# Attention stages: a third score buffer, the maxima reordered on VectorE and the exponentials reordered on ScalarE

## The chip, the cores and the metric

The kernel runs on one core of a Trainium2 chip. The metric is device time in microseconds of one execution. TensorE, VectorE (DVE), ScalarE (ACT), GpSimd (POOL) and SyncE (SP) each run their own instruction queue in order and meet at semaphores.

## The reference, cut to what matters

Two transformer blocks are applied to 512 latent tokens of width 1024, the first with 256 context tokens beside them. All is float32. Four attentions are computed: a neighbourhood attention in each layer of the first block (with an attention among the context tokens in the first layer only), then a differential attention and a forgetting attention in the second block.

```python
# neighbourhood: local keys with a bias table, and all 256 context keys
s_loc = einsum('bjqhd,bjkhd->bhjqk', q_r, k_loc) * scale + bias
p = softmax(concatenate([s_loc, s_ctx], -1), -1)
out = p[..., :n_loc] @ v_loc + p[..., n_loc:] @ v_ctx
# differential: 8 heads, two softmaxes each, causal
logits = einsum('bqhmd,bkhmd->bhmqk', qb, k) * scale + bias
p = softmax(where(rel >= 0, logits, -inf)); w = p[:, :, 0] - lam * p[:, :, 1]
o = rms_norm(w @ v, subln_g) * (1 - lambda_init)
# forgetting: 16 heads, causal, with a decay that is added to the scores
logits = einsum('bqhd,bkhd->bhqk', qb, k) * scale + decay
out = softmax(where(causal, logits, -inf)) @ v
```

Around them stand projections, a gated recurrence, expert layers and dense layers with matrices of 1024 by up to 5632.

## The kernel before, in words

All four attentions are built by one function, `attention` (line 1260). Its work is cut into units. A unit is 128 queries of two heads (or of the two halves of one differential head), against nk keys. In the neighbourhood stages nk is 512 in 12 units per layer, and the first layer has six more units, for the context tokens, with nk of 256. The differential and the forgetting stages have 32 units each; nk goes 128, 256, 384, 512, 512, 384, 256, 128 and again, so that 8 units are one cycle.

One unit goes through these steps:

1. scores (TensorE, L1295), into one of two pairs of PSUM banks. Unit u+2 waits until VectorE has taken the scores of unit u.
2. maxima (VectorE): the `pre` of the stage (L1453 and L1454; L2692 and L2694; L2875 and L2878) moves the scores with their bias into the score buffer S, then L1384 reduces them to a negated maximum.
3. exponentials (ScalarE, L1345), in place in S, with their sum.
4. transposes (TensorE, L1306), in one or two rounds of up to four tiles of 128x128. Round 0 goes into one PSUM bank, round 1 into another. Each round waits until the copies of the preceding unit have emptied its bank.
5. copies (ScalarE, L1362), one per round, from PSUM to the buffer ET.
6. product with the values (TensorE, L1323 with L1326, or L1330 in the differential stage). L1326 also spreads the reciprocals of the sums (VectorE, L1390).
7. output: ScalarE copies the spread reciprocals (L1354) and VectorE multiplies (L1408). In the differential stage VectorE does both steps itself (L2698, L2699).

The order of each queue is written out by hand. TensorE does, for each u: transposes of u, scores of u+2, product of u-1. ScalarE does: copies of u, exponentials of u+1, reciprocal copy of u-1, then the extra work of the stage. VectorE does: reciprocals of u-1, maxima of u+1, output of u-2, then the extra work.

Only the differential stage has extra work, for the norm over each head. After the fourth unit of a head VectorE clamps that head's outputs (`on_dve`, L2749) for unit u-4; ScalarE squares them (`on_act`, `squares`, L2724) for unit u-3, and waits for the clamp. ScalarE then takes roots (L2729 to L2731) every second head and scales the finished outputs (`scaled`, L2737, four instructions per head) in two later places.

Of the kernel before, what the change touches and what calls it, by code (L numbers as in the profile page):

```python
# [22 lines left out]
P = 128  # L23
D = 1024
KT = D // P
NLAT, NCTX = 512, 256
NTOK = NLAT + NCTX
# [7 lines left out]
LOCAL = 2 * NA_ROWS * BLOCK  # L35
BIAS_KINDS = 3
BIAS_PAIR = HEADS_PER_TILE * BIAS_KINDS * LOCAL
# [170 lines left out]
def build(nc, wtile, wahead, wmod, wshift, conds, params, consts, rope, onehot, biases, x_in, out, dbg=None, dbg_name="X", upto=99, limit=10 ** 9):  # L208
    with ExitStack() as ctx:
# [8 lines left out]
        X = sb_split("X", KT * NTOK)  # L218
        H = sb_split("H", 8192)
        ring = sb_split("ring", SLOTS * TILE)  # L220
        PB = sb_split("PB", 23552)
# [15 lines left out]
        bank = [psum[:, 512 * i:512 * i + 512] for i in range(8)]  # L237
# [81 lines left out]
        ident = cn("ident", 0, P)  # L319
# [940 lines left out]
        def attention(units, S, ET, stats, sc_sets, turn_banks, odd_on_act=False, outputs=None):  # L1260
# [4 lines left out]


            n = len(units)
            NS = len(sc_sets)
            B = lambda s, k=n: s.reserve(k)
            b_sr, b_tk = B(scores_ready), B(scores_taken)  # L1270
            b_mx, b_ex, b_or, b_oc = B(max_ready), B(exp_ready), B(out_ready), B(out_copied)
# [11 lines left out]
            scale = lambda u: small[:, u % 2 * P:(u % 2 + 1) * P]  # L1283
            mx = lambda u: stats[:, 2 * u:2 * u + 2]
            sm = lambda u: stats[:, 2 * (n + u):2 * (n + u) + 2]
            Sv = lambda u: S[u % 2][:, 0:2 * units[u]["nk"]].rearrange("p (m k) -> p m k", m=2)
            copied = lambda r, u: (probsT_copied.sem, b_ca + n_a[u] + r // 2 + 1) if r % 2 == 0 else (hidT_copied.sem, b_cd + n_d[u] + r // 2 + 1)

            def scores(eng, u):
# [8 lines left out]
            def ten(eng, ready, values):  # L1298
                def turn(u):
                    eng.wait_ge(exp_ready.sem, b_ex + u + 1)  # L1300
                    for r, tiles in enumerate(rounds(u)):
                        ready, before = ((probsT_ready, n_a[u]), (hidT_ready, n_d[u]))[r % 2]
                        if before + r // 2:
                            eng.wait_ge((probsT_copied, hidT_copied)[r % 2].sem, (b_ca, b_cd)[r % 2] + before + r // 2)
                        for t in tiles:
                            mm = nc.tensor.transpose(bank[tb[r % 2]][:, (t % 4) * P:(t % 4) * P + P], S[u % 2][:, t * P:(t + 1) * P], ident)  # L1306
                        mm.then_inc(ready.sem, 1)

                def product(u):
                    if u < 0:  # L1310
                        return
                    for r in range(len(rounds(u))):
                        eng.wait_ge(*copied(r, u))
                    if u >= 2:
                        eng.wait_ge(out_copied.sem, b_oc + u - 1)
                    if u == 0:
                        values(eng)
                    nt, w = units[u]["nk"] // P, units[u]["width"]
                    probs = lambda m, t: ET[u % 2][:, (m * nt + t) * P:(m * nt + t + 1) * P]
                    if turned[u]:  # L1320
                        for t in range(nt):
                            for m in range(2):
                                nc.tensor.matmul(ob(u)[64 * m:64 * m + 64, 0:P], units[u]["pv"](m, t), probs(m, t), start=(t == 0), stop=(t == nt - 1))  # L1323
                        eng.wait_ge(recip_ready.sem, b_rc + u + 1)
                        for m in range(2):
                            mm = nc.tensor.matmul(ob(u)[64 * m:64 * m + 64, P:2 * P], sm(u)[:, m:m + 1].broadcast_to([P, DH]), ident, start=True, stop=True)  # L1326
                    else:
                        for m in range(2):
                            for t in range(nt):
                                mm = nc.tensor.matmul(ob(u)[:, m * w:(m + 1) * w], probs(m, t), units[u]["pv"](m, t), start=(t == 0), stop=(t == nt - 1))  # L1330
                    mm.then_inc(out_ready.sem, 1)
                ready(eng)
                scores(eng, 1)
                for u in range(n):
                    turn(u)
                    scores(eng, u + 2)
                    product(u - 1)
                product(n - 1)
# [9 lines left out]
            def sca(eng):  # L1348
                def copy_scale(u):
                    if u >= 0 and turned[u]:  # L1350
                        if u >= 2:
                            eng.wait_ge(out_copied.sem, b_oc + u - 1)
                        eng.wait_ge(out_ready.sem, b_or + u + 1)
                        nc.scalar.copy(scale(u), ob(u)[:, P:2 * P]).then_inc(scale_copied.sem, 1)  # L1354
                for u in range(n):
                    for r, tiles in enumerate(rounds(u)):
                        if r % 2 == 0 or odd_on_act:
                            ready, copied_, first = ((probsT_ready, probsT_copied, b_ta + n_a[u]), (hidT_ready, hidT_copied, b_td + n_d[u]))[r % 2]
                            eng.wait_ge(ready.sem, first + r // 2 + 1)
                            if u >= 2:  # L1360
                                eng.wait_ge(out_ready.sem, b_or + u - 1)
                            nc.scalar.copy(ET[u % 2][:, tiles[0] * P:(tiles[-1] + 1) * P], bank[tb[r % 2]][:, 0:len(tiles) * P]).then_inc(copied_.sem, 1)  # L1362
                    exponentials(eng, u + 1)
                    copy_scale(u - 1)
                    if outputs is not None and u >= 3:
                        outputs[0](eng, u - 3)
                copy_scale(n - 1)
                if outputs is not None:
                    for u in range(n - 3, n):
                        outputs[0](eng, u)  # L1370
                    outputs[2](eng)

            def maxima(eng, u):
                if u >= n:
                    return
                if u >= 2:
                    if n_a[u - 1]:
                        eng.wait_ge(probsT_ready.sem, b_ta + n_a[u - 1])
                    if n_d[u - 1]:
                        eng.wait_ge(hidT_ready.sem, b_td + n_d[u - 1])  # L1380
                eng.wait_ge(scores_ready.sem, b_sr + u + 1)
                units[u]["pre"](eng, Sv(u), sets(u)).then_inc(scores_taken.sem, 1)
                eng.wait_ge(scores_taken.sem, b_tk + u + 1)
                nc.vector.tensor_reduce(mx(u), Sv(u), AX, ALU.max, negate=True).then_inc(max_ready.sem, 1)  # L1384

            def vec(eng):
                for u in range(n + 2):
                    if 1 <= u <= n:
                        eng.wait_ge(exp_ready.sem, b_ex + u)
                        nc.vector.reciprocal(sm(u - 1), sm(u - 1)).then_inc(recip_ready.sem, 1)  # L1390
                    if u < n:
                        maxima(eng, u + 1)
                    if u < n:
                        for r, tiles in enumerate(rounds(u)):
                            if r % 2 and not odd_on_act:
# [4 lines left out]
                    if u >= 2:  # L1400
                        x = u - 2
                        w = units[x]["width"]
                        eng.wait_ge(out_ready.sem, b_or + x + 1)
                        if turned[x]:
                            eng.wait_ge(scale_copied.sem, b_sc + n_t[x] + 1)
                            dst = units[x]["dst"]
                            flat = (lambda ap: ap) if len(dst.shape) == 2 else (lambda ap: ap.rearrange("p (r c) -> p r c", c=BLOCK))
                            ins = nc.vector.tensor_tensor(dst, flat(ob(x)[:, 0:P]), flat(scale(x)), ALU.mult)  # L1408
                        else:
                            eng.wait_ge(recip_ready.sem, b_rc + x + 1)  # L1410
                            ins = units[x]["out"](eng, ob(x)[:, 0:2 * w].rearrange("p (m e) -> p m e", m=2), sm(x))
                        ins.then_inc(out_copied.sem, 1)
                    if outputs is not None and u >= 4:
                        outputs[1](eng, u - 4, b_oc + u - 3)
                if outputs is not None:
# [5 lines left out]
            return (lambda eng: scores(eng, 0)), (lambda eng: exponentials(eng, 0)), (lambda eng: maxima(eng, 0)), run  # L1421


        SN = [PB[:, 2 * NTOK:2 * NTOK + 4 * LOCAL], X[:, 2 * BIAS_PAIR:2 * BIAS_PAIR + 4 * LOCAL]]
        EN = [PB[:, 4 * NTOK:4 * NTOK + 4 * LOCAL], H[:, KT * NTOK:KT * NTOK + 4 * LOCAL]]
        far_banks = lambda bs: psum[:, 512 * bs[0]:512 * bs[0] + 1024].rearrange("p (m k) -> p m k", m=2)[:, :, LOCAL:LOCAL + NCTX]
        two_banks = lambda bs, nk: psum[:, 512 * bs[0]:512 * bs[0] + 1024].rearrange("p (m k) -> p m k", m=2)[:, :, 0:nk]
# [1235 lines left out]

        QK2 = lambda i: PB[:, i * NLAT:(i + 1) * NLAT]
        V2 = PB[:, 8192:8192 + 4096].rearrange("p (t n) -> p t n", t=4)
        S3 = [PB[:, 16384 + b * 2 * NLAT:16384 + (b + 1) * 2 * NLAT] for b in range(2)]
        ET3 = [PB[:, 18432 + b * 2 * NLAT:18432 + (b + 1) * 2 * NLAT] for b in range(2)]
        BT2 = PB[:, 20480:20480 + 2048].rearrange("p (h n) -> p h n", h=A_HEADS)
        OTOK = H[:, 0:4096].rearrange("p (j n) -> p j n", j=4)
        SQ = H[:, 4096:4608].rearrange("p (j n) -> p j n", j=4)  # L2670
        KV = PB[:, 11776:11776 + 8192]
        O4 = PB[:, 4096:8192].rearrange("p (k t) -> p k t", k=KT)
        S4 = [PB[:, 8192 + b * 2 * NLAT:8192 + (b + 1) * 2 * NLAT] for b in range(2)]
        ET4 = [PB[:, 20480 + b * 2 * NLAT:20480 + (b + 1) * 2 * NLAT] for b in range(2)]
        FK = [PB[:, 22528:23552].rearrange("p (h k) -> p h k", h=2), H[:, 0:(B_HEADS - 2) * NLAT].rearrange("p (h k) -> p h k", h=B_HEADS - 2)]
        FQ = X[:, NLAT:NLAT + 4 * B_HEADS].rearrange("p (j h) -> p j h", j=4)
# [442 lines left out]
```

## Time and profile before

| | us |
|---|---|
| median of 3 runs | 3840.16 (3836.74 to 3841.09) |
| profiled execution, its own time | 3846.45 |
| its span, first to last instruction | 3844.7 |
| TensorE busy | 3605.9 (94%) |
| VectorE busy | 2157.3 (56%) |
| ScalarE busy | 1569.2 (41%) |
| chain that ended last | TensorE 83%, DVE 6%, ACT 4%, DMA 3%, issue 2% |

The four attention stages take some 287 us of the span together. In the views, a row of instructions has its busy time and the idle time of its engine just before it, with what released it. PE is TensorE's matmul queue.

### The profile page before, as it was taken

How to read it: one execution, taken by the hardware profiler on the slowest of the kernel's cores; microseconds unless marked ns; L12 is line 12 of the kernel's file. 1: busy time of each engine (PE TensorE's matmuls, PEld its weight loads, DVE VectorE, ACT ScalarE, POOL GpSimd, SP SyncE). 2: the span in 40 equal slices, each digit the busy share in tenths (PEclk: the TensorE clock that was granted, in tenths of full speed). 3: DMA queues.
4: the chain of work that ended last, by engine and by line, in shares of the span. 5: the costliest groups of instructions: out<-in, count | busy, mean ns of one | idle time of the engine just before them, and what ended most of it. 6: DMA issues, size and time to landing. Idle time of an engine off the chain costs nothing.

```text
span 3844.7 us, 51787 instructions
## 1 busy us (share of the span) xinstructions
PE 3605.9 (94%) x19796; PEld 2766.0 (72%) x19796; DVE 2157.3 (56%) x3269; ACT 1569.2 (41%) x2667; POOL 307.0 (8%) x410
## 2 busy tenths in 40 slices
PE   8998897999999687999999998999999999889998
PEld 7886574666788454556888776788878887667887
DVE  7867845987785773337763346666234333664332
ACT  3336634988423762113222346322233222553222
POOL 0110001100111002001210000111000001000001
PEclk9999578999999668999999999999999999999999
DMA  7552013998456017996773210576323223312222
GB/s 276 175 172 97 2 61 128 373 349 315 164 203 189 1 45 273 406 405 240 271 245 107 99 61 17 191 235 204 103 88 137 93 99 104 132 39 88 98 97 74
DMA packets 166268, 620.69 MB, mean 161 GB/s; under 512 B 19116, under 2 KB 20741, under 8 KB 164893
## 3 DMA queue, kind: packets, MB, share of 16 engines
q1 hardware_dynamic: 114928, 420.58, 30.3%
q0 software_dynamic: 46880, 169.11, 13.3%
q10 hardware_dynamic: 4238, 27.90, 1.9%
q8 instruction: 157, 2.57, 0.3%
q14 instruction: 65, 0.53, 0.0%
HBM read 596.74 MB, written 17.88 MB: 160 GB/s over the span
## 4 chain that ended last, share of the span: by engine, by line
PE 83%; DVE 6%; ACT 4%; DMA 3%; issue 2%; SPq 0%; POOL 0%; DVEq 0%; ACTq 0%; POOLq 0%
PE psum L2594 24%; PE psum L886 13%; PE psum L2608 13%; PE psum L983 5%; PE psum L2200 4%; PE psum L1059 4%; PE psum L813 3%; DMA ring<-wtile 2%; PE psum L2431 2%; PE psum L2219 2%; PE psum L2450 1%; PE psum L1306 1%; PE psum L1295 1%; PE psum L821 1%; PE psum L1585 1%
## 5 line engine op out<-in xcount | busy, mean ns | idle before, releaser
L837 ACT CAST small_r<-ring 128x1024 fp32r<-128x1024 f32 x263 | 275.0, 1048 | 1034.8 <-PE psum L886 336.4
L841 DVE TENSOR_TENSOR ring_r<-ring,small_r 128x1024 fp32r<-128x1024 f32 x264 | 322.7, 1224 | 645.6 <-ACT small_r L837 645.3
L837 ACT CAST PB_r<-ring 128x1024 fp32r<-128x1024 f32 x247 | 256.4, 1049 | 544.1 <-PE psum L2594 325.2
L841 DVE TENSOR_TENSOR ring_r<-ring,PB_r 128x1024 fp32r<-128x1024 f32 x248 | 299.5, 1222 | 246.8 <-ACT PB_r L837 246.3
L2594 PE MATMUL psum<-H_r,ring_r 128*128 128x512 f32 x1344 | 336.2, 392 | 0.0
L2594 PE MATMUL psum<-H_r,small_r 128*128 128x512 f32 x1344 | 326.9, 395 | 0.0
L2594 PE MATMUL psum<-H_r,PB_r 128*128 128x512 f32 x1344 | 318.6, 389 | 0.0
L2594 PEld LDWEIGHTS psum<-H_r,small_r 128*128 128x128 f32 x1344 | 252.3, 188 | 61.2
L2594 PEld LDWEIGHTS psum<-H_r,ring_r 128*128 128x128 f32 x1344 | 252.2, 188 | 56.0
L2594 PEld LDWEIGHTS psum<-H_r,PB_r 128*128 128x128 f32 x1344 | 252.3, 188 | 53.4
L886 PE MATMUL psum<-H_r,small_r 128*128 128x512 f32 (+1 forms) x944 | 251.8, 365 | 0.0
L886 PEld LDWEIGHTS psum<-H_r,small_r 128*128 128x128 f32 x944 | 159.0, 188 | 32.5 <-issue 1.8
L2608 PE MATMUL psum<-PB_r,ring_r 128*128 128x512 f32 x704 | 177.3, 392 | 0.0
L2608 PE MATMUL psum<-PB_r,small_r 128*128 128x512 f32 x704 | 171.9, 395 | 0.0
L886 PE MATMUL psum<-X_r,small_r 128*128 128x512 f32 x624 | 170.8, 344 | 0.0
L2608 PE MATMUL psum<-PB_r 128*128 128x512 f32 x704 | 167.7, 389 | 0.0
L886 PE MATMUL psum<-H_r,ring_r 128*128 128x512 f32 (+1 forms) x784 | 160.3, 353 | 0.0
L2634 DVE TENSOR_TENSOR small<-small,psum 128x512 f32<-128x512 f32 x88 | 60.5, 688 | 172.8 <-PE psum L2594 171.3
L2608 PEld LDWEIGHTS psum<-PB_r,small_r 128*128 128x128 f32 x704 | 132.1, 188 | 32.0
L2608 PEld LDWEIGHTS psum<-PB_r,ring_r 128*128 128x128 f32 x704 | 132.1, 188 | 29.3
L2608 PEld LDWEIGHTS psum<-PB_r 128*128 128x128 f32 x704 | 132.1, 188 | 28.2
L886 PEld LDWEIGHTS psum<-H_r,ring_r 128*128 128x128 f32 x784 | 128.2, 188 | 21.8
(472 smaller groups left out, 6561.5 us busy)
## 6 DMA issues: line engine op xcount, KB each, us to landing
ring<-wtile SPq DMA_DIRECT2D x776, 512.0 KB, 5.4
spare<-wmod POOLq DMA_DIRECT2D x97, 512.0 KB, 4.7
H<-wmod POOLq DMA_DIRECT2D x48, 512.0 KB, 4.5
PB<-wmod POOLq DMA_DIRECT2D x48, 512.0 KB, 4.4
X<-wmod POOLq DMA_DIRECT2D x47, 512.0 KB, 5.1
PB<-wahead POOLq DMA_DIRECT2D x16, 512.0 KB, 7.9
h_rows<-PB POOLq DMA_DIRECT2D x10, 512.0 KB, 4.4
PB<-wmod SPq DMA_DIRECT2D x4, 1024.0 KB, 15.2
```

The source lines that it names most:

```text
L813: nc.tensor.matmul(out(j, w)[:, 0:e - a], halves[j][z][:, k * P:(k + 1) * P], src[1][0](k, a, e), start=(x == 0 and z == 0), stop=False)
L837: copy(high(j), slot(g0 + j)).then_inc(high_ready.sem, 1)
L841: nc.vector.tensor_tensor(low(g0 + j), slot(g0 + j), high(j).bitcast(F32), ALU.subtract).then_inc(low_ready.sem, 1)
L886: mm = nc.tensor.matmul(bank[b + w][:, 0:e - a], w_part[:, k * P:(k + 1) * P], src[1][x](k, a, e), start=(not last and k == 0 and x == 0), ...
L983: mm = nc.tensor.matmul(bank[ob(c, t)][:, 0:width], src[1][x](2 * q + k, t * P, (t + 1) * P), w_part[:, 512 * k:512 * k + width], start=(j ...
L1059: mm = nc.tensor.matmul(bank[2 * (j % 2) + w][:, 0:e - a], w_part[:, k * P:(k + 1) * P], parts_at[1][x](k, a, e), start=(not last and k == ...
L2200: mm = nc.tensor.matmul(bank[2 + s][0:M, :], XG[x][:, 2 * q + k, 0:M], w_part[:, 512 * k:512 * k + 512], start=(not low and q == 0 and k = ...
L2219: mm = nc.tensor.matmul(bank[6 + s][0:M, :], HIDT[x][:, f, 0:M], w_part[:, 512 * s:512 * s + 512], start=(not low and f == 0 and x == 0), ...
L2431: mm = nc.tensor.matmul(bank[2 + s][M * o:M * o + M, 0:HALF], XG[e % 2][:, 2 * q + k, :], w[:, EXP_DIM * k + HALF * o:EXP_DIM * k + HALF * ...
L2594: mm = nc.tensor.matmul(bank[2 * (p % 2) + z][:, :], w_part[:, k * P:(k + 1) * P], SLIM[1][x](k, 0, NLAT), start=(not last and k == 0 and ...
L2608: mm = nc.tensor.matmul(bank[4 + j % 2][:, :], w_part[:, k * P:(k + 1) * P], HID2[x][:, kk * NLAT:(kk + 1) * NLAT], start=(not last and kk ...
L2634: nc.vector.tensor_tensor(SGF[p % 2], SGF[p % 2], bank[2 * (p % 2) + 1][:, :], ALU.mult).then_inc(prod_ready.sem, 1)
```

## The change

Four things are changed. Nothing else differs, and the count of compute instructions is the same.

- The score buffer S has three parts in place of two, in all four stages. The maxima of unit u then wait for the transposes of unit u-3, not u-2, before they write S.
- VectorE's maxima of unit 1 stand ahead of its loop. In the loop the maxima of u+1, which stood behind the reciprocals and ahead of the output of u-2, are replaced by those of u+2, behind that output and ahead of the stage's extra work.
- ScalarE's exponentials of u+1 stand ahead of its copies of u. They stood behind them.
- TensorE's order is the same: only the buffer that its transposes read is picked by `u % NB`.

```diff
-            NS = len(sc_sets)
+            NS, NB = len(sc_sets), len(S)
...
-            Sv = lambda u: S[u % 2][:, 0:2 * units[u]["nk"]].rearrange("p (m k) -> p m k", m=2)
+            Sv = lambda u: S[u % NB][:, 0:2 * units[u]["nk"]].rearrange("p (m k) -> p m k", m=2)
...
                 for u in range(n):
+                    exponentials(eng, u + 1)
                     for r, tiles in enumerate(rounds(u)):
...
-                    exponentials(eng, u + 1)
                     copy_scale(u - 1)
...
-                if u >= 2:
-                    if n_a[u - 1]:
-                        eng.wait_ge(probsT_ready.sem, b_ta + n_a[u - 1])
-                    if n_d[u - 1]:
-                        eng.wait_ge(hidT_ready.sem, b_td + n_d[u - 1])
+                if u >= NB:
+                    if n_a[u - NB + 1]:
+                        eng.wait_ge(probsT_ready.sem, b_ta + n_a[u - NB + 1])
+                    if n_d[u - NB + 1]:
+                        eng.wait_ge(hidT_ready.sem, b_td + n_d[u - NB + 1])
...
             def vec(eng):
+                maxima(eng, 1)
                 for u in range(n + 2):
                     if 1 <= u <= n:
                         eng.wait_ge(exp_ready.sem, b_ex + u)
                         nc.vector.reciprocal(sm(u - 1), sm(u - 1)).then_inc(recip_ready.sem, 1)
-                    if u < n:
-                        maxima(eng, u + 1)
...
                         ins.then_inc(out_copied.sem, 1)
+                    maxima(eng, u + 2)
                     if outputs is not None and u >= 4:
                         outputs[1](eng, u - 4, b_oc + u - 3)
...
-        SN = [PB[:, 2 * NTOK:2 * NTOK + 4 * LOCAL], X[:, 2 * BIAS_PAIR:2 * BIAS_PAIR + 4 * LOCAL]]
+        SN = [PB[:, 2 * NTOK:2 * NTOK + 4 * LOCAL], X[:, 2 * BIAS_PAIR:2 * BIAS_PAIR + 4 * LOCAL], X[:, 2 * BIAS_PAIR + 4 * LOCAL:2 * BIAS_PAIR + 8 * LOCAL]]
...
-        S3 = [PB[:, 16384 + b * 2 * NLAT:16384 + (b + 1) * 2 * NLAT] for b in range(2)]
+        S3 = [PB[:, a:a + 2 * NLAT] for a in (16384, 16384 + 2 * NLAT, 12288)]
...
-        S4 = [PB[:, 8192 + b * 2 * NLAT:8192 + (b + 1) * 2 * NLAT] for b in range(2)]
+        S4 = [PB[:, 8192 + b * 2 * NLAT:8192 + (b + 1) * 2 * NLAT] for b in range(3)]
```

## Rows read from the trace of the kernel before

**Rows 1.** Windows of the four attention stages: length, busy time of each engine, clock.
```profile
316.28:372.30 56.02, 53.14 (x588) 40.42 (x588) 40.98 (x80) 42.95 (x118) 1.34 (x2) 0.97 0.23 79
1242.60:1284.30 41.70, 39.75 (x458) 31.79 (x456) 30.82 (x56) 31.48 (x80) 0.00 (x0) 0.96 0.15 50
2268.00:2364.00 96.00, 87.91 (x604) 64.90 (x604) 80.28 (x197) 73.95 (x259) 0.00 (x0) 0.96 0.02 7
3315.50:3409.00 93.50, 77.55 (x730) 50.86 (x728) 78.42 (x186) 65.51 (x204) 0.00 (x0) 0.98 0.11 44
```

**Rows 2.** Timeline, neighbourhood stage, first layer: start, duration, engine, line, idle before.
```profile
326.90 0.73 ACT L1345 ACTIVATE X<-X,spare 128x512 f32<-128x512 f32 x1
...
328.23 0.20 ACT L1345 ACTIVATION_READ_ACCUMULATOR X<-X,spare 128x1 f32 x1
...
328.59 1.09 PE L1306 MATMUL psum<-con,X 128*128 128x128 f32 x8
...
329.29 1.07 ACT L1362 COPY H<-psum 128x512 f32<-128x512 f32 x2 [0.31 <-PE psum L1306]
...
329.62 1.15 PE L1295 MATMUL psum<-PB,H 64*128 64x128 f32 x12
...
330.24 0.73 ACT L1345 ACTIVATE PB<-PB,spare 128x512 f32<-128x512 f32 x1
...
330.91 0.69 DVE L1453 TENSOR_SCALAR X<-psum 128x512 f32<-128x512 f32 x1 [0.46 <-PE psum L1295]
...
332.24 1.22 DVE L1384 TENSOR_REDUCE spare<-X 128x2 f32<-128x1024 f32 x1
...
333.59 0.73 ACT L1345 ACTIVATE X<-X,spare 128x512 f32<-128x512 f32 x1
```

**Rows 3.** Windows: four context units, one differential cycle, one forgetting cycle.
```profile
360.61:369.89 9.28, 7.75 (x79) 5.12 (x77) 5.70 (x15) 7.20 (x25) 0.00 (x0) 1.00 0.01 3
2317.55:2340.45 22.90, 21.46 (x155) 16.04 (x153) 20.38 (x52) 19.57 (x73) 0.00 (x0) 1.00 0.00 1
3340.91:3362.95 22.04, 19.29 (x185) 12.59 (x185) 20.05 (x49) 16.55 (x52) 0.00 (x0) 1.00 0.01 1
```

**Rows 4.** Groups by line in the forgetting cycle: count, busy, mean ns, idle before.
```profile
L1345 ACT ACTIVATE PB<-PB,spare 128x128 f32<-128x128 f32 (+3 forms) x16 | 8.9, 557 | 1.5 <-DVE spare L1384 1.5
L2875 DVE SCALAR_TENSOR_TENSOR PB<-H,X,psum 128x256 f32<-128x256 f32 (+3 forms) x16 | 8.0, 541 | 1.4 <-PE psum L1295 1.2
L1384 DVE TENSOR_REDUCE spare<-PB 128x2 f32<-128x256 f32 (+3 forms) x8 | 6.6, 820 | 0.3
...
L1306 PE MATMUL psum<-con,PB 128*128 128x128 f32 x41 | 6.4, 285 | 2.8 <-ACT PB L1345 2.6
...
L1362 ACT COPY PB<-psum 128x512 f32<-128x512 f32 (+1 forms) x12 | 5.8, 516 | 3.3 <-PE psum L1306 3.1
L2878 DVE TENSOR_TENSOR PB<-PB,con 128x256 f32<-128x256 f32 x9 | 3.8, 425 | 0.3
```

**Rows 5.** Timeline of the forgetting stage: a late load, and a unit with nk of 128.
```profile
3327.01 1.41 DVE L2875 SCALAR_TENSOR_TENSOR PB<-H,X,psum 128x512 f32<-128x512 f32 x2 [2.92 <-DMA H<-frow_save]
...
3342.72 0.44 PE L1306 MATMUL psum<-con,PB 128*128 128x128 f32 x2
...
3343.09 0.92 PE L1295 MATMUL psum<-PB 64*128 64x384 f32 x4
...
3359.05 0.49 PE L1295 MATMUL psum<-PB 64*128 64x128 f32 x4
```

**Rows 6.** Groups by line in the differential cycle (columns as in the forgetting cycle).
```profile
L2694 DVE SCALAR_TENSOR_TENSOR PB<-psum,PB 128x512 f32<-128x512 f32 (+1 forms) x9 | 5.6, 621 | 0.2
...
L2724 ACT ACTIVATE H<-H 128x128 f32<-128x128 f32 x9 | 2.7, 296 | 0.2
...
L2692 DVE TENSOR_SCALAR PB<-psum,PB 128x256 f32<-128x256 f32 (+1 forms) x4 | 2.4, 598 | 0.0
...
L2749 DVE TENSOR_SCALAR H<-H 128x512 f32<-128x512 f32 x2 | 0.8, 422 | 0.0
```

More of the change, by code:

```diff
@@ L1305, in turn @@
                         for t in tiles:
-                            mm = nc.tensor.transpose(bank[tb[r % 2]][:, (t % 4) * P:(t % 4) * P + P], S[u % 2][:, t * P:(t + 1) * P], ident)
+                            mm = nc.tensor.transpose(bank[tb[r % 2]][:, (t % 4) * P:(t % 4) * P + P], S[u % NB][:, t * P:(t + 1) * P], ident)
                         mm.then_inc(ready.sem, 1)
```

## The prediction

> **What bounds the kernel now.** I read the windows of the four attention stages first. They last 56.0, 41.7, 96.0 and 93.5 us [rows 1]; the change touches nothing else, so 287 of 3844.7 us are at stake. TensorE is busy for 95%, 95%, 92% and 83% of them, VectorE for 73% to 84%, ScalarE for 70% to 77%. No engine is full, so the period of a unit is set by loops of waits through several engines, and the sum has to be made over these loops.
>
> The timeline of the neighbourhood stage shows them [rows 2]. The reader is to see three things in it.
>
> First, the period: exponentials start at 326.90, 330.24 and 333.59, one unit every 3.34 us.
>
> Second, a loop over one unit. The exponentials start at 326.90 and end at 328.43 (1.53). The transposes start 0.16 later, at 328.59. The copies start 0.70 behind them, at 329.29. The next exponentials start 0.95 behind the start of the copies, at 330.24. The sum is 3.34, the period itself. The copies stand in this loop because the exponentials are queued behind them. Call it loop A.
>
> Third, a loop over two units, B: scores, maxima, exponentials, transposes, scores. Maxima from 330.91 to 332.24+1.22=333.46 take 2.55; 0.13 later the exponentials start, at 333.59, though 0.04 would do as I read it from the shortest gaps. Exponentials take 1.53, then 0.16 to the transposes; from there 1.03 to the scores (328.59 to 329.62); scores take 1.15 and 0.14 pass to the maxima (329.62+1.15=330.77 to 330.91). That is 2.55+0.04+1.53+0.16+1.03+1.15+0.14=6.60 for two units, 3.30 per unit. Loop A is longer than B by only 0.04 per unit.
>
> **The change part by part.** *Third buffer and the maxima's wait.* The removed wait is for the transposes of u-2. But the scores of u are issued on TensorE behind the transposes of u-2, and the maxima need these scores anyway. The wait that ends last there is for the scores (0.46 us for L1295) [rows 2], so the buffer gives nothing: 0. It would give something only if TensorE's scores were issued earlier, and their order is unchanged. At the worst it costs nothing either, as it adds no instruction.
>
> *Maxima one place on.* Written as one sequence, VectorE did output u-2, reciprocals u, maxima u+2, output u-1. Now it does output u-2, maxima u+2, reciprocals u, output u-1. Only the reciprocals of u (0.15) and the extra work change sides. The maxima no longer wait for the exponentials of u, but they wait for the scores of u+2, which come behind the transposes of u, which wait for the same exponentials. So nothing is gained: 0. The reciprocals are late by one set of maxima; they are needed only at the end of the product of u, behind the transposes of u+1 and the scores of u+3, over 2 us later. Covered: 0. The extra work of the differential stage is priced below.
>
> *Exponentials ahead of the copies.* Loop A is cut: the exponentials no longer stand behind the copies. But now the copies of u-1 stand behind the exponentials of u. The transposes of u write the bank that these copies empty, so they wait for exponentials of u and then for the first copy of u-1. That lengthens loop B by a copy. This is the step that the prediction rests on.
>
> Neighbourhood stages: the copies' queue slot begins 1.42 to 1.43 behind the start of the exponentials (the read of the sum overlaps by 0.1), and two copies take 1.07 [rows 2], so one about 0.59, then 0.16 to TensorE as before: 2.17 in place of 1.53+0.16=1.69, +0.48. Loop B is 7.08, or 3.54 per unit against 3.34: +0.20. With 10 to 11 periods of full width per layer that is +2.1 per layer, +4.2 for both. Bounds: 0, if the copy starts before the exponentials do in some way that I don't see; +5.9 per layer if both copies (1.07) come into the loop. I take the first copy alone, because the second bank's transposes come half a microsecond later too. The six context units have a period of 9.28/4=2.32 [rows 3], and a chain with narrower terms; I take 0 for them, between -1 and +1.
>
> Forgetting stage, in cycles of 8 units, 22.04 us each [rows 3]. Loop B passes over every second unit, so over a cycle it holds half of each group. Exponentials 8.9/2=4.45; L2875 8.0/2=4.0; L2878 4x0.425=1.7, with 0.07 of gaps per unit 0.3; reduction 6.6/2=3.3; copies one per unit 4x0.516=2.1 [rows 4]. Transposes up to the scores 1.03 for 8 tiles [rows 2] and 0.37 for 2 (3342.72 to 3343.09) [rows 5], on average 0.70, x4=2.8. Scores 1.13 to 1.15 at the widest [rows 2] and 0.49 at the narrowest [rows 5], on average 0.81, x4=3.25. Handovers 0.15+0.04+0.10 per unit, x4=1.15. The sum is 23.05 against 22.04: +1.0 per cycle. Without the copy it would be about 21, below the present period, which shows that loop A bounds now. The stage has another brake: VectorE waits 2.92 us for a load at 3327 [rows 5], which comes at its own time and swallows what was lost before. That leaves 28 of 32 units, 3.5 cycles: +3.4. Bounds: 0; and +6.6 if the second copies count too (another 0.9 per cycle).
>
> Differential stage, 22.90 us per cycle [rows 3]. The same sum: exponentials 4.45, L2694 and L2692 together 4x0.92=3.7 (8 of the one, 4 of the other, 4.97+2.39=7.36, halved), reduction 3.3, copies 2.1, transposes 2.9, scores 3.25, handovers 1.15: 20.85. That alone would not bound. But here the extra work meets the new order. Squares of a finished head stand on ScalarE, in the iteration u=4h+3, and wait for the clamp on VectorE; the clamp now stands behind the maxima of u+2, and the exponentials of that same unit u+2=4h+5 stand behind the squares. So each head puts clamp and squares in series into loop B, always in the odd units: 0.42 less an overlap of 0.09, 0.04 of handover, and 4x0.296=1.18 [rows 6], together 1.55, twice per cycle: 3.1. One of the two sets of scalings per cycle (four instructions, taken at the length of the squares, 1.2) falls ahead of an odd unit's exponentials too. 20.85+3.1+1.2=25.15 against 22.90, and against 22.6 in a cycle without scalings: +2.4 per cycle, x3.5=+8.5. Bounds: +0, if squares find their operand in time; +12, if even units are held as well.
>
> *Sum:* 4.2+3.4+8.5=+16.1 us. The stages follow one another on TensorE and nothing runs beside them that could swallow it. Against the profiled execution that is 3846.45+16.1=3862.6. The median of the runs shown is 6.3 lower, so **3856.3**.
>
> **The rivals.** *Faster.* TensorE waits for the exponentials ahead of its transposes, 2.6 us per forgetting cycle [rows 4]. If the new order lets them start sooner and the bank is free in time, most of it goes: 2.6x3.5=9.1, and about as little again in the other stages, where TensorE is nearly full [rows 1]. With 10 us gained the time is 3830. It decides where the exponentials of u are done before the transposes of u-1 end, so that the copies of u-1 are never held. For it: VectorE and ScalarE have slack. Against: the maxima end only 0.13 us before the exponentials start now [rows 2], so they cannot start sooner. The Trainium skill, "Perfetto Trace Analysis", section Optimization Strategy, says that a gap that repeats on the engine that should be full can mean too few buffers for the next tile. By that rule the third buffer would bring this rival's 3830; what the trace shows before the gap is the exponentials, not a buffer.
>
> *Absorbed.* The copy's place matters less than the loop says, because waits overlap: within 4 us of before, 3842.
>
> *Bank only.* The copy costs what I say, the squares do not: +4.2+3.4 and up to 3 in the differential stage, 3849. It decides if the clamp is done by the time ScalarE's queue reaches the squares.
>
> *More.* The longer waits of TensorE lower its granted clock in parts of a stage. It is at 1.00 in three steady stretches in spite of waits [rows 3], and 0.96 to 0.98 over whole stages [rows 1], so against it. If half a cycle of each of the two long stages ran at 1.2 GHz, some 11 us would be added: 3867. The Trainium skill, "TensorE: Matmul & The Clock Gate", section "A second HAM failure mode: psum-queue depth-cycling", tells of such a fall between short bursts of matmuls.
>
> **How the numbers follow.** Forecast 0.56, bank only 0.19, more 0.08, absorbed 0.09, faster 0.08. The forecast's own range is 3850 to 3863. Below 3844 lie faster and most of absorbed, above 3867 half of the last: 3844 to 3867. About 0.2%, 7.7 us, is what a measurement can tell from no change: slower by more, 3847.9 and above, holds the forecast, more and most of bank only, 0.81; the same 0.11; faster 0.08.
>
> **What would show it.** In the neighbourhood stage the exponentials should start every 3.54 us on average over two units, and the transposes should follow the end of a copy, not of the exponentials. A forgetting cycle should last 23.0, a differential cycle 25.2. ScalarE should wait for L2749 ahead of L2724 twice per cycle. If TensorE's transposes start with no ScalarE wait, or the differential cycle stays below 23, the prediction is wrong. The rest of the kernel should keep its times.

## The result and the profile after

The changed kernel takes 3859.47 us (median of 5 runs, 3848.28 to 3864.54), the kernel before 3840.16 (5 runs, 3836.74 to 3844.6). The ratio is 1.0045, with a 95% interval of 1.0029 to 1.0061: slower by 11 to 23 us. The forecast was 3856.3. The profiled execution took 3863.77 us, with a span of 3862.0; forecast for it was 3862.6.

The windows of the four attention stages, now cut in the same way at rows of transposes (in the forgetting stage a little past the last), answer to [rows 1]; the columns are the same.

```profile
317.96:373.88 55.92, 50.13 (x551) 38.38 (x549) 40.13 (x77) 40.08 (x113) 0.27 (x1) 0.97 0.21 73
1244.01:1283.97 39.96, 36.35 (x411) 28.66 (x409) 30.08 (x53) 28.37 (x75) 0.00 (x0) 0.96 0.16 55
2276.61:2376.50 99.89, 85.57 (x589) 63.48 (x588) 78.34 (x186) 69.81 (x244) 0.00 (x0) 0.97 0.01 1
3330.05:3425.00 94.95, 77.96 (x730) 51.27 (x728) 78.55 (x187) 63.27 (x203) 0.00 (x0) 0.96 0.10 41
```

Measured in the same way in both traces, from the start of the first row of transposes to the start of the last, the stages took:

| us | neighbourhood 1 | neighbourhood 2 | differential | forgetting | sum |
|---|---|---|---|---|---|
| before | 52.5 | 38.1 | 90.5 | 91.5 | 272.6 |
| changed | 55.9 | 40.0 | 99.9 | 93.2 | 289.0 |
| difference | +3.4 | +1.9 | +9.4 | +1.7 | +16.4 |
| forecast | +2.1 | +2.1 | +8.5 | +3.4 | +16.1 |

The span grew by 17.3, so 0.9 lies elsewhere, and that is a small sum of larger things that have nothing to do with the change (see the last section). That the sums agree to 0.3 us is luck: the stages are off by +1.1, +0.9 and -1.7 (the two neighbourhood stages taken together).

The timeline of the neighbourhood stage in the changed kernel answers to [rows 2]. L1363 are the copies, L1362 before.

```profile
336.24 0.72 ACT L1345 ACTIVATE X<-X,spare 128x512 f32<-128x512 f32 x1 [0.95 <-DVE spare L1384]
...
337.67 1.04 ACT L1363 COPY PB<-psum 128x512 f32<-128x512 f32 x2
...
338.38 1.06 PE L1306 MATMUL psum<-con,X 128*128 128x128 f32 x8 [0.21 <-ACT PB L1363]
...
339.37 1.15 PE L1295 MATMUL psum<-PB,H 64*128 64x128 f32 x12
...
339.65 0.72 ACT L1345 ACTIVATE PB<-PB,spare 128x512 f32<-128x512 f32 x1 [0.77 <-DVE spare L1384]
...
340.67 0.69 DVE L1453 TENSOR_SCALAR X<-psum 128x512 f32<-128x512 f32 x1 [0.79 <-PE psum L1295]
```

The reader is to see the new loop B. Exponentials start at 336.24, the copies of the unit before them 1.43 later, and the transposes at 338.38, released by the copy and no longer by the exponentials: 2.14 behind the start of the exponentials, where it was 1.69 and the forecast 2.17. Scores follow 0.99 later, the maxima at 340.67. And ScalarE waits for the maxima, 0.95 and 0.77 us: it did not wait for them before, as its copies filled that time.

Three cycles as in [rows 3]: one of the forgetting stage, and the second and third of the differential stage.

```profile
3356.38:3379.36 22.98, 19.05 (x185) 12.58 (x185) 20.06 (x49) 16.06 (x53) 0.00 (x0) 1.00 0.01 1
2300.43:2325.70 25.27, 21.37 (x154) 16.04 (x153) 20.41 (x50) 17.30 (x63) 0.00 (x0) 1.00 0.01 1
2325.70:2352.55 26.85, 22.96 (x154) 16.71 (x153) 20.65 (x52) 19.54 (x71) 0.00 (x0) 0.94 0.00 1
```

Forecast were 23.0 and 25.2. The groups by line of the forgetting cycle answer to [rows 4].

```profile
L1345 ACT ACTIVATE PB<-PB,spare 128x256 f32<-128x256 f32 (+3 forms) x16 | 8.8, 554 | 6.4 <-DVE spare L1384 6.4
...
L1306 PE MATMUL psum<-con,PB 128*128 128x128 f32 x41 | 6.3, 280 | 4.1 <-ACT PB L1363 3.8
...
L1363 ACT COPY PB<-psum 128x512 f32<-128x512 f32 (+1 forms) x12 | 5.6, 498 | 0.0
```

TensorE waits 3.8 us per cycle for copies, where it waited 2.6 for exponentials. The copies wait for nothing, since they are queued behind exponentials that outlast the transposes. The exponentials wait 6.4 us for maxima in place of 1.5. In the second differential cycle, with the two lines in question:

```profile
L1306 PE MATMUL psum<-con,PB 128*128 128x128 f32 x40 | 5.8, 275 | 3.9 <-ACT PB L1363 3.9
...
L2724 ACT ACTIVATE H<-H 128x128 f32<-128x128 f32 x8 | 2.4, 297 | 3.0 <-DVE H L2749 3.0
```

ScalarE's squares wait 3.0 us per cycle for the clamp; before it was 0.2 [rows 6].

### The profile page after: what moved, and what is told of

It reads as the page before. It is cut to its first block, busy times and chain, and to the rows that moved or that the text cites. A ratio compares the mean times of both kernels' runs of the same rounds, so it can differ in the third digit from the quotient of the medians.

```text
span 3862.0 us, 51782 instructions
## 1 busy us (share of the span) xinstructions
PE 3600.8 (93%) x19796; PEld 2763.4 (72%) x19796; DVE 2158.9 (56%) x3269; ACT 1564.4 (41%) x2667; POOL 310.1 (8%) x410
## 4 chain that ended last, share of the span: by engine, by line
PE 81%; DVE 7%; ACT 5%; DMA 4%; issue 2%; SPq 0%; DVEq 0%; POOL 0%; ACTq 0%; POOLq 0%
PE psum L2594 24%; PE psum L886 13%; PE psum L2608 13%; PE psum L983 5%; PE psum L1059 4%; PE psum L2200 4%; DMA ring<-wtile 3%; PE psum L813 3%; PE psum L2431 2%; PE psum L2219 2%; PE psum L1295 1%; PE psum L2450 1%; PE psum L1306 1%; PE psum L821 1%; DVE spare L1384 1%
```

## The experiments

My theory has two parts. The first copy, put behind the exponentials, lengthens the loop over two units (loop B). The clamp, put behind the maxima, holds squares and with them exponentials in the differential stage. The rivals give it all to one of the two orders, to the buffer, or to ScalarE's load. Whole times of one kernel scatter by 10 us and more (before: 3833 to 3856 in 31 runs). From the second cycle on, a cycle repeats to 0.01 us between the two traces of the kernel before; in the changed kernel the third differential cycle, in which TensorE's clock fell, was 26.85 and 26.48. So the verdicts rest on cycles. In the fences below, the windows are six neighbourhood periods (five where the text says so), a differential cycle (the second, or the second and the third) and a forgetting cycle, as far as shown, with the columns of [rows 3]. The repeat of the kernel before is the yardstick; it comes first.

**The kernel before again.**

> The kernel before once more, for the scatter of its parts between executions: cycles 3.35, 22.9 and 22.04 us again to 0.1 us; if TensorE's clock rises at another time in the first recurrence, that part differs by several us with nothing changed.

```profile
333.77:353.85 20.08, 20.08 (x243) 16.06 (x241) 16.67 (x31) 16.50 (x42) 0.00 (x0) 1.00 0.01 2
2302.05:2324.66 22.61, 21.45 (x154) 16.04 (x153) 20.09 (x52) 17.31 (x63) 0.00 (x0) 1.00 0.01 2
2324.66:2347.56 22.90, 21.46 (x154) 16.04 (x153) 20.38 (x52) 19.56 (x73) 0.00 (x0) 1.00 0.00 1
3350.17:3372.20 22.03, 19.29 (x186) 12.59 (x185) 20.05 (x49) 16.55 (x52) 0.00 (x0) 1.00 0.01 1
```

Periods of 20.08/6=3.35, cycles of 22.61, 22.90 and 22.03: the same to 0.01, in an execution that was 8 us longer as a whole (3854.13).

**VectorE's part alone.** The diff is against the changed kernel, as in all that follow but where said.

```diff
                 for u in range(n):
-                    exponentials(eng, u + 1)
                     for r, tiles in enumerate(rounds(u)):
...
+                    exponentials(eng, u + 1)
                     copy_scale(u - 1)
```

> The change without its ScalarE part: exponentials of u+1 behind the copies of u again; third buffer and VectorE's new order kept. Theory of the two loops: loop A is back and bounds the neighbourhood and forgetting stages as before, 3.34 us per unit of full width and 22.0 per forgetting cycle. In the differential stage the clamp still stands behind the maxima of u+2, so squares wait: the cycle between 24 and 26 us, total 6 to 9 us above before. Rival 'ScalarE's order is all of it': differential cycle 22.6 to 22.9, total as before within 2 us.

```profile
2283.16:2308.53 25.37, 21.68 (x155) 16.08 (x154) 20.33 (x50) 17.51 (x63) 0.00 (x0) 1.00 0.01 1
```

Six neighbourhood periods take 20.08 us and the forgetting cycle 22.04, as before. The second differential cycle is 25.37, the third 26.31 (25.27 and 26.85 in the changed kernel): nearly all of its differential loss, with ScalarE's order as before. The ratio of the whole is 1.0017 (1.0003 to 1.0030), 1 to 12 us, with 6 to 9 expected. The rival that ScalarE's order is all of it is out.

**ScalarE's part alone.**

```diff
             def vec(eng):
-                maxima(eng, 1)
...
+                    if u < n:
+                        maxima(eng, u + 1)
...
                         ins.then_inc(out_copied.sem, 1)
-                    maxima(eng, u + 2)
```

> The change without its VectorE part: maxima of u+1 in their old place; third buffer and the exponentials ahead of the copies kept. Theory of the two loops: neighbourhood 3.5 per unit and forgetting 23.0 per cycle as in the changed kernel; differential 23.3 to 24.2 per cycle, as the clamp stands in its old place; total about 11 above before. Rival 'the maxima's order is all of it': 3.34, 22.9 and 22.0, total as before within 2 us. Rival 'the ScalarE order alone costs as much as the whole change': differential cycle 25 or more, total 16 above.

```profile
331.97:353.05 21.08, 20.32 (x240) 16.04 (x241) 16.75 (x31) 15.83 (x43) 0.00 (x0) 1.00 0.01 4
2293.82:2317.02 23.20, 21.42 (x154) 16.04 (x153) 20.25 (x52) 17.02 (x63) 0.00 (x0) 1.00 0.01 1
...
3341.37:3364.35 22.98, 19.05 (x184) 12.58 (x185) 19.80 (x49) 16.04 (x53) 0.00 (x0) 1.00 0.00 1
```

21.08/6=3.51 and 22.98: the whole loss of the neighbourhood and forgetting stages comes from ScalarE's order. The second differential cycle is 0.6 above before, a bit below the 23.3 that I gave as the low end; the third is 23.60. The whole time is a miss: ratio 0.9997 (0.9982 to 1.0013), at most 5 us slower, where I expected 11. The stages of its trace add up to 9.4 us more than before (54.3, 42.5, 91.6 and 93.6), of which some 3 are in the start of the second stage. Where the rest of the whole time gives that back was not found; the scatter of its other parts is as large.

**The third buffer alone.** Both orders put back as in the two runs above.

> The third score buffer alone, both orders as before. Theory: nothing, since the scores come behind the same transposes that free the buffer: 3.34, 22.9 and 22.0 us, total as before but for the scatter of the clock in the recurrence. Rival 'the buffer's place in memory costs': single instructions of L1384, L1345 or L1306 longer than 1220, 714 and 273 ns in their widest forms and the cycles longer by that. Rival 'buffer helps': cycles shorter by 0.2 us or more.

```profile
331.50:351.58 20.08, 20.08 (x243) 16.06 (x241) 16.67 (x31) 16.52 (x42) 0.00 (x0) 1.00 0.02 7
2283.87:2306.48 22.61, 21.45 (x154) 16.04 (x153) 20.09 (x52) 17.32 (x63) 0.00 (x0) 1.00 0.01 1
...
3331.45:3353.48 22.03, 19.29 (x186) 12.59 (x184) 19.69 (x48) 16.56 (x52) 0.00 (x0) 1.00 0.01 1
```

Nothing, to 0.01 us, in these windows; the ratio is 0.9995 (0.9982 to 1.0007). The next cycle of either stage is a little longer than before, 23.02 against 22.90 and 22.39 against 22.04; why was not looked into. None is shorter.

**The changed kernel with the clamp ahead of the maxima.**

```diff
-                    maxima(eng, u + 2)
                     if outputs is not None and u >= 4:
                         outputs[1](eng, u - 4, b_oc + u - 3)
+                    maxima(eng, u + 2)
```

> The changed kernel with VectorE's extra work of the differential stage (the clamp, L2749) ahead of the maxima of u+2 in place of behind. Theory: the squares no longer wait for a whole set of maxima, the differential cycle falls from 26.8 to 23.3 to 24.2; neighbourhood and forgetting stages as in the changed kernel, 3.5 and 23.0; total about 11 above before, 6 below the changed kernel. Rival 'the squares do not matter, only the copy behind the exponentials': the differential cycle stays at 25 to 27 and the total at that of the changed kernel.

The second and third differential cycle (the forgetting cycle is 22.99, as in the changed kernel):

```profile
2292.84:2315.99 23.15, 21.44 (x155) 16.05 (x154) 20.21 (x51) 17.03 (x63) 0.00 (x0) 1.00 0.01 1
2315.99:2339.56 23.57, 21.42 (x154) 16.04 (x153) 20.68 (x52) 19.66 (x73) 0.00 (x0) 1.00 0.00 1
```

One moved line takes the stage from 99.9 to 91.6 us; the squares' wait for the clamp falls from 3.0 us in the second cycle to 0.8. So the clamp's place costs 8.3 us. Against the given trace of the kernel before, 1.1 would be left for the copy behind the exponentials, but that trace ran at half clock at the start of this stage, and its repeat did not:

```profile
2270.57:2277.30 6.73, 6.30 (x21) 3.00 (x20) 4.34 (x9) 3.35 (x10) 0.00 (x0) 0.52 0.00 0
2279.10:2285.80 6.70, 5.10 (x30) 2.67 (x28) 5.59 (x10) 4.03 (x12) 0.00 (x0) 1.00 0.01 4
```

The first differential cycle took 24.36 us in the one and 22.97 in the other. By the cycles the copy costs 0.5 to 0.7 (23.15 against 22.61, 23.57 against 22.90), an estimate of some 2 us for 3.5 cycles. The ratio to before is 1.0005 (0.9990 to 1.0020), -4 to +8 us, where I expected 11: a miss, as with ScalarE's part alone.

**The first copy ahead of the exponentials.** This tells the first copy from ScalarE's load.

```diff
                 for u in range(n):
-                    exponentials(eng, u + 1)
...
                             nc.scalar.copy(ET[u % 2][...], bank[tb[r % 2]][...]).then_inc(copied_.sem, 1)
+                            if r == 0:
+                                exponentials(eng, u + 1)
```

> The changed kernel with one thing moved: ScalarE's exponentials of u+1 stand between the first and the second copy of u, in place of ahead of both. VectorE's order, the clamp behind the maxima, TensorE's order and the third buffer are as in the changed kernel. Theory that the first copy behind the exponentials is what lengthens loop B: neighbourhood back to 3.34 us per unit, forgetting cycle to 22.0 or a little less; the differential cycle keeps the cost of the clamp and stays at 24.5 to 26. Rival 'it is ScalarE's load or any copy behind the exponentials': 3.5 and 23.0 stay.

```profile
333.94:354.02 20.08, 20.08 (x243) 16.06 (x241) 16.59 (x31) 16.85 (x43) 0.00 (x0) 1.00 0.01 2
2296.33:2321.25 24.92, 21.74 (x154) 16.03 (x153) 20.32 (x50) 17.52 (x63) 0.00 (x0) 1.00 0.00 1
...
3350.39:3372.22 21.83, 19.34 (x186) 12.55 (x184) 19.96 (x49) 16.60 (x52) 0.00 (x0) 1.00 0.01 2
```

3.35, and 21.83, 0.2 below before: with one copy moved past the exponentials the loss is gone, and the differential stage keeps the clamp's (24.92, then 25.89). Both parts of the theory stand. This kernel was executed once (3854.16 us), so its whole time says nothing.

**Scores ahead of the transposes.** The theory says what the third buffer could be good for: loop B runs through the scores only because TensorE issues them behind the transposes. The clamp stands ahead of the maxima here.

```diff
                 for u in range(n):
-                    turn(u)
                     scores(eng, u + 2)
+                    turn(u)
                     product(u - 1)
```

> The changed kernel with the clamp ahead of the maxima, and on TensorE the scores of u+2 issued ahead of the transposes of u in place of behind them. Theory: this is what the third buffer and the early maxima lacked. Loop B (scores, maxima, exponentials, copy, transposes, scores) is cut, as the scores wait only until VectorE has taken those of u. Neighbourhood 3.1 to 3.25 us per unit in place of 3.51, forgetting cycle 21.0 to 21.5 in place of 22.98, differential 22.2 to 22.8 in place of 23.6; in all about 9 us below the kernel before. Rival 'the copies behind the exponentials bound by themselves, whatever TensorE does': cycles stay at 3.5, 23.0 and 23.6.

```profile
332.59:349.32 16.73, 16.73 (x202) 13.38 (x200) 14.15 (x25) 13.68 (x36) 0.00 (x0) 1.00 0.02 6
2291.73:2313.99 22.26, 20.58 (x154) 15.94 (x153) 19.75 (x50) 16.96 (x63) 0.00 (x0) 1.00 0.01 2
...
3337.15:3358.28 21.13, 19.37 (x187) 12.54 (x185) 19.81 (x49) 15.77 (x52) 0.00 (x0) 1.00 0.01 2
```

The differential and the forgetting cycle fall below the kernel before: 22.26 and 21.13. The neighbourhood period does not. The first window holds five periods, 16.73/5=3.35, where I expected 3.1 to 3.25. TensorE is busy for all of it, as it is for all of the 20.08 us of the kernel before, so it is the bound in both. The exponentials are now far ahead of it:

```profile
333.37 0.19 ACT L1345 ACTIVATION_READ_ACCUMULATOR X<-X,spare 128x1 f32 x1
...
335.94 1.09 PE L1306 MATMUL psum<-con,X 128*128 128x128 f32 x8
```

They end at 333.56, 2.38 us before the transposes that read them (0.16 in [rows 2]), and the period is the same. What the neighbourhood stages gain (49.3 against 52.5 us for the first) lies in the first units and in the last two of full width, which take 2.90 us each there. The ratio is 0.9981 (0.9967 to 0.9995).

**The same with the exponentials between the copies.** The diff is against the run just told of.

```diff
                 for u in range(n):
-                    exponentials(eng, u + 1)
...
                             nc.scalar.copy(ET[u % 2][...], bank[tb[r % 2]][...]).then_inc(copied_.sem, 1)
+                            if r == 0:
+                                exponentials(eng, u + 1)
```

> As the run with the scores first, but ScalarE's exponentials of u+1 stand between the first and the second copy of u. Theory: the first copy is never held by exponentials, and in the differential and forgetting stages that gains: cycles 21.8 to 22.3 and 20.8 to 21.3; in the neighbourhood stage the copy comes back into the path, 3.2 to 3.3 us per unit; in all about 10 us below the kernel before. Rival: the two places are alike, as every wait is covered once the scores come first; all cycles within 0.1 of those of the run with the scores first.

```profile
2286.81:2308.57 21.76, 20.82 (x154) 15.90 (x152) 19.75 (x50) 17.32 (x65) 0.00 (x0) 1.00 0.01 2
...
3329.70:3350.38 20.68, 19.54 (x186) 12.50 (x184) 19.55 (x49) 15.96 (x52) 0.00 (x0) 1.00 0.01 2
```

0.5 less per cycle in both causal stages. The neighbourhood period is again 3.35, with TensorE busy throughout (3.2 to 3.3 expected). Median 3829.79, ratio 0.9970 (0.9954 to 0.9985): 6 to 18 us below before.

**Scores first in the kernel before.** The diff is against the kernel before; the third buffer is added as in the change.

```diff
-            NS = len(sc_sets)
+            NS, NB = len(sc_sets), len(S)
...
                 for u in range(n):
-                    turn(u)
                     scores(eng, u + 2)
+                    turn(u)
```

> The kernel before with three buffers and TensorE's scores of u+2 ahead of the transposes of u; ScalarE and VectorE in their old orders. Theory: loop A (exponentials behind the copies, copies behind the transposes) is not cut: the neighbourhood stage stays at 3.33 to 3.35 us per unit; the forgetting cycle falls to 21.3 to 21.7, as VectorE no longer waits for scores; total 3 to 5 us below before. Rival 'loop B bounded alone, so that scores first is enough': neighbourhood 3.1 to 3.25.

```profile
332.18:348.92 16.74, 16.74 (x203) 13.39 (x201) 13.84 (x25) 13.21 (x35) 0.00 (x0) 1.00 0.03 12
```

Five neighbourhood periods of 3.35, as expected, but this does not show loop A: TensorE is busy for all of the 16.74 us, so its own work sets the period here too. The forgetting cycle is 21.16, the second differential cycle 21.79. The ratio is 0.9973 (0.9958 to 0.9988); 3 to 5 us were expected and 5 to 16 were measured. So most of the gain comes with TensorE's order, without the changed orders of the other two.

**The better place in each stage.** Exponentials ahead of both copies in the neighbourhood stages, between them elsewhere. The diff is against the run with the exponentials between.

```diff
                 for u in range(n):
+                    if not between:
+                        exponentials(eng, u + 1)
...
-                            if r == 0:
+                            if r == 0 and between:
                                 exponentials(eng, u + 1)
```

> Scores first and the clamp first in all stages; exponentials ahead of both copies in the neighbourhood stages, between the copies in the differential and forgetting stages. Theory: each stage as in the better of the two runs before: first transposes to last 49.3, 35.6, 84.2 and 85.8 us; that is 1.4 us below the run with the exponentials between everywhere, about 14 below the kernel before in the stages, of which the whole time shows 9 to 15. Rival: stages lean on one another, the first one's gain is taken back in the expert stage, and the whole time is that of the run with the exponentials between.

The stages lasted 49.3, 35.6, 84.1 and 87.0 us, 16.6 below the kernel before. The ratio is 0.9976 (0.9963 to 0.9989), no better than with the exponentials between everywhere. The two can't be told apart by their whole times, and either beats both given kernels.

**The changed kernel again.**

> The changed kernel once more, for the scatter of its parts and for its time beside the others on one chip. Theory: cycles again 3.51, 25.3 to 26.9 and 22.98 us; whole time 12 to 20 above before. The first expert stage, 384.6 us in the changed kernel's trace and 378.0 in that of before, differs by chance (383.4 in the repeat of before), so it may be anything between 374 and 385 here.

```profile
2303.99:2329.26 25.27, 21.37 (x154) 16.04 (x153) 20.41 (x50) 17.28 (x63) 0.00 (x0) 1.00 0.00 1
2329.26:2355.74 26.48, 23.00 (x154) 16.92 (x153) 20.67 (x52) 19.54 (x71) 0.00 (x0) 0.94 0.00 1
```

Six neighbourhood periods take 21.08 us (3.51 each) and the forgetting cycle 22.99. Ratio 1.0042 (1.0027 to 1.0056): the slowdown repeats.

## Why the prediction was right

*What bounds.* For the neighbourhood stages "No engine is full" was wrong. The 95% is an average over the stage; in its steady stretch TensorE is busy for 20.08 of 20.08 us, and one unit of its own work takes 3.35. The step of 0.16 from the exponentials to the transposes is more than the handover: TensorE was still busy then, and the profile shows no idle time before these transposes. Where it did stand idle until the exponentials were done, the step is 0.05, as here in the forgetting stage of the kernel before (3331.50+0.19=3331.69 to 3331.74):

```profile
3331.50 0.19 ACT L1345 ACTIVATION_READ_ACCUMULATOR PB<-PB,spare 128x1 f32 x1
...
3331.74 1.96 PE L1306 MATMUL psum<-con,PB 128*128 128x128 f32 x8 [3.35 <-ACT PB L1345]
```

With 0.05 loop A is 3.23 long and loop B 3.25 per unit, both below TensorE's 3.35. The forecast was not hurt, since it took loop B from the measured period, which is the same number whatever sets it. In the forgetting stage TensorE does wait for exponentials, 2.6 us per cycle, so loops bound there; that it is loop A and not B was summed, not tried apart. The step that the prediction rests on was right: with the copy in it, loop B is the bound. It was forecast at 3.54 per unit and is 3.51, and the rows of the changed kernel add up to it (2.14+0.99+1.30 to the maxima, 2.55 for them, 0.03: 7.01 for two units).

*Third buffer: 0.* Shown: its neighbourhood period is that of before, and from the second cycle on, no cycle of the run with it alone is shorter than before. All kernels with the scores first have it too; how much of their gain needs it was not tried apart.

*Maxima one place on: 0.* Shown for the neighbourhood and forgetting stages by the run with VectorE's part alone.

*Copy behind the exponentials.* Neighbourhood +4.2 forecast, +5.3 measured, of which the steady part is 0.17 per period and the rest lies in the first units, whose length differs between executions of one kernel by up to 2.6 us (39.96 and 42.56 for the second stage of the changed kernel). The bound of +5.9 per layer for both copies was too wide: by its own terms it is 4.6. Forgetting +1.0 per cycle forecast, +0.94 measured. But the stage lost 1.7, not 3.4. The wait for the late load fell from 2.92 us [rows 5] to 1.08:

```profile
3341.43 1.41 DVE L2875 SCALAR_TENSOR_TENSOR PB<-H,X,psum 128x512 f32<-128x512 f32 x2 [1.08 <-DMA H<-frow_save]
```

So 1.8 us lost ahead of the load were swallowed, as the prediction says. But the cycle with the load in it also became shorter, 26.3 us in place of 27.2. From the load to the end of that cycle, in the kernel before, in the changed kernel, and in the kernel with the third buffer alone:

```profile
3327.01:3342.72 15.71, 12.31 (x125) 8.89 (x121) 12.38 (x32) 9.38 (x31) 0.00 (x0) 0.89 0.00 0
3341.43:3356.38 14.95, 12.42 (x137) 8.99 (x133) 12.63 (x32) 11.02 (x38) 0.00 (x0) 1.00 0.01 2
3317.20:3331.45 14.25, 11.22 (x125) 7.97 (x125) 12.39 (x32) 9.69 (x32) 0.00 (x0) 1.00 0.00 0
```

In the kernel before TensorE waited 3.35 us behind the load, and then ran at the lower clock: its next eight transposes, the row shown above, took 1.96 us, against 1.09 in [rows 2]. The repeat of the kernel before has the same fall (15.70 us, 0.89). The kernel with the buffer alone has the old orders and no fall there, and its cycle with the load takes 25.6. Against that one the changed order costs 0.7 us in this cycle (26.3). With 0.94 in each of the next two cycles and 0.7 in the last, which is cut short, that is 3.3, an estimate of what the stage loses at equal clock. So the sum was right; the fall that the kernel before has here, and the changed kernel does not, hid half of it.

*Differential.* +8.5 forecast, +9.4 measured, and moving the clamp is shown to give 8.3 back. The sum had errors that the total hides. I took clamp, squares and scalings into loop B over a copy that alone "would not bound" (20.85), so the copy's share should have been nothing with the clamp in its old place; it is 0.5 to 0.7 per cycle, some 2 us. The half clock at the start of the kernel before takes 1.4 off the difference. And the third cycle is 1.6 above the second (0.3 in the kernel before), which was not in the sum: TensorE's clock fell (next section but one). It fell once more in the fourth. The rival called more was thus partly right, in the place that it named, for some 1 us in the third cycle; what it took in the fourth was not measured apart.

*The rivals.* Faster: the exponentials did start no sooner, as said. The Trainium skill ("Perfetto Trace Analysis", section Optimization Strategy) says that a gap that repeats on the engine that should be full can mean too little SBUF or PSUM for the next tile. The gap that repeats on TensorE in the forgetting cycle, 2.6 us, stayed 2.6 when the SBUF buffer alone was added, and the cycle fell from 22.04 to 21.16 when TensorE's order was changed as well; more PSUM banks were not tried. More: TensorE's clock did fall, in the third and fourth differential cycle. Bank only: it is the run with the clamp first, where the differential cycle stays 0.5 to 0.7 above before.

## What to carry to other kernels

When an instruction is moved ahead in one engine's queue, look at what is now behind it, and whether a buffer that another engine needs is emptied there: here one copy of 0.5 us behind the exponentials cost 0.17 us per unit. Write down each loop of waits with its length before reordering, and beside them the time that each engine's own work takes in one period of the steady stretch, not averaged over the stage: here loops of 3.23 and 3.25 us stood beside 3.35 us of TensorE, and no reordering took the steady period below that. A third buffer alone gave nothing, because the scores were issued no earlier; with the scores ahead of the transposes the two causal cycles fell. And before a difference of a few us is given to the change, look at the granted clock of both traces at that place.

## What the runs showed of the hardware

TensorE's granted clock decides several microseconds of the whole time outside the attentions. The two windows of 20 us at the end of the first recurrence, in the kernel before and then in the changed one, with TensorE's busy time, clock, DMA share and GB/s:

```profile
480.00:500.00 20.00, 19.70 (x222) 0.50 0.04 10
500.00:520.00 20.00, 19.64 (x225) 0.50 0.38 151
```

```profile
480.00:500.00 20.00, 19.32 (x254) 0.58 0.01 2
500.00:520.00 20.00, 16.62 (x276) 0.93 0.40 159
```

Both run there at 1.2 GHz from before 420 us on. In the changed kernel the clock rises to 2.4 GHz before 500 us, in the kernel before behind 520, and the part from the last row of transposes to the last small matmul of the recurrence takes 139.1 and 147.6 us. The repeat of the changed kernel has 147.5 and the buffer run 139.8, so it is not the change. The first expert stage, from the output projection to its end, takes 374 to 385 us over the thirteen traces, in no order that I can see. Between the two given traces the first gives 8.5 back and the second takes 6.6 (378.0 to 384.6), so they nearly cancel.

In the differential stage of all four traces with the clamp behind the maxima, the clock falls for a short while in the third cycle (0.93 to 0.94); in those with the clamp in its old place or first it stays at 1.00 there. In both traces of the changed kernel it falls again in the fourth cycle, here in the given one:

```profile
2352.55:2376.60 24.05, 20.55 (x137) 15.26 (x136) 18.31 (x46) 18.42 (x66) 0.00 (x0) 0.93 0.00 1
```

In the third cycle of the changed kernel it looks so:

```profile
2329.64 0.98 PE L1306 MATMUL psum<-con,PB 128*128 128x128 f32 x4 [2.08 <-ACT PB L1363]
...
2330.56 2.08 PE L1295 MATMUL psum<-PB 64*128 64x512 f32 x4
...
2334.14 1.13 PE L1295 MATMUL psum<-PB 64*128 64x512 f32 x4
```

TensorE waited 2.08 us, the next widest scores took 2.08 us and those of the unit after them 1.13. The clamp's place thus costs twice, once by its wait and once by the clock. The stages' first units differ between executions for the same reason: the given kernel before starts its differential stage at 0.52 and its repeat at 1.00 (first differential cycles 24.36 and 22.97).
